# Where the last four parts of a modulation are computed: beside the chunked linear attention or beside the latent attention

## The chip, the cores and the metric

The kernel runs on one core of a Trainium2 chip. Its engines work side by side and meet through semaphores: PE (TensorE) multiplies matrices into PSUM, DVE (VectorE) and ACT (ScalarE) work element by element, POOL (GpSimd) does so too and issues some transfers, SP (SyncE) issues nearly all transfers. The metric is the time of one execution in microseconds; lower is better.

## What the kernel computes

Two transformer blocks over 512 tokens of width 1024. Only the first block matters here. Its modulation turns a vector `c` into six parts of 1024 values:

```python
sc = jax.nn.silu(c)
shift1, scale1, gate1, shift2, scale2, gate2 = jnp.split(sc @ w_mod + b_mod, 6, axis=-1)
h = modulate(rms_norm(x, norm1_g), shift1, scale1)
y, yc = token_mixer(h, hc, P, last)
x = x + gate1[:, None, :] * y
h = modulate(rms_norm(x, norm2_g), shift2, scale2)
x = x + gate2[:, None, :] * grouped_moe(h, ...)
```

`shift1` and `scale1` are needed before the token mixer, the last four parts (`gate1`, `shift2`, `scale2`, `gate2`) only after it. The token mixer has three branches: a gated linear attention, computed in chunks of 64 tokens in both directions with 4 heads; a softmax attention of 8 heads whose 512 queries see 512 + 256 keys (the latent attention); and a long convolution (hyena). A mixture of 16 experts follows, which gathers tokens into slots.

## The kernel before

The kernel is a chain of stages. Each stage is one block with an instruction list for each engine, written out by hand; every engine must have ended its list before the next stage starts. The stages that matter here, in order, with the time at which PE starts each in the profile: the first two parts of the modulation (`mod_stage`, 0), the projections of the linear attention (`gla_project_stage`, 43 us), its chunks (`gla_chunk_stage`, 165.6 us), keys, queries and values (`qk_stage`, 241.2 us), the latent attention (`latent_attention_stage`, 346.5 us) and the projections of the hyena (`hyena_project_stage`, 488.3 us).

**Weights.** `Ring` (line 49) holds four slots of 1 MB. `plan_block1` (line 3788) lists the chunks in the order of their use; SP loads chunk k once chunk k − 4 has been used. `issue_until(sp, n)` issues the list up to chunk n. A stage issues its own chunks and some of the next stage's. In the plan of before, 16 chunks named `mod2` (the last four parts of `w_mod`) stand between the query chunks and the hyena chunks.

**Split weights.** For most projections a weight chunk is split into two rounded parts: ACT copies it (`Split.high`, line 118, recorded on line 124) and POOL subtracts the copy from the chunk (`Split.low`, line 126, recorded on line 130). PE waits for the second. In `groups_stage` these are done ahead for the following group, and for the first chunks of the stage after it: `leave=1` leaves one of the two next chunks to the following stage, `leave=2` both.

**The rest of the modulation.** `LaterMods` (line 432) works in 8 groups of 512 columns. It is called with a step number a. On PE, at a mod 4 = 0 and 1, four matmuls each multiply a chunk (`mod_products`, line 316) into PSUM bank 7; at a mod 4 = 3 four small matmuls turn the row into columns (`mod_turn`, line 323). Between them ACT copies the row out of PSUM (line 463, at a mod 4 = 2); after them DVE adds the bias (line 473, at the next a mod 4 = 0). The first product of a group waits for DVE's sum of the group before (`added`), since both use the same bank. Before, this ran in the latent attention, with its steps numbered as that stage's own: one step to each of 32 blocks of 128 queries.

**The chunk stage.** First, for four pairs of direction and heads, PE multiplies chunk states (lines 263 and 1242) and DVE carries the state from chunk to chunk (lines 1316, 1321, 1326). Then come 16 heads, that is 4 token tiles by 4 heads. For head a PE computes scores (`scores(a)`, line 1255); DVE masks them (line 1333); PE computes outputs (`outputs(a)`, lines 1268 and 1274); ACT squares them (line 1299); DVE takes mean and reciprocal (lines 1342 and 1345); ACT takes the root (line 1302); DVE scales by it (line 1348) and multiplies by the gate (line 1352). `scores` runs one head ahead of `outputs`; `outputs(a)` waits until head a − 2 is done. At the end PE transposes all heads (line 1290) and ACT copies the result (line 1305). Beside this, SP wrote zeros into `h_slots`, the slots of the experts (16 transfers of 512 KB), from a region that DVE had cleared (line 1311).

**The latent attention.** For block a PE computes scores (line 1393), DVE takes the maximum (line 1442) and the bias (line 1448), ACT the exponential (line 1421), DVE normalises block a − 1 (line 1455), PE transposes block a − 2 (line 1403), DVE copies the transposes out (line 1463), and after each fourth block PE multiplies by the values (line 263) and ACT copies (line 1430).

Of the kernel before, what the change touches and what calls it, by code (L numbers as in the profile page):

```python
# [14 lines left out]
D = 1024  # L15
# [7 lines left out]
RING = 4  # L23
# [15 lines left out]
C_KV, C_GK, C_GV, C_GA = 0, 512, 768, 1280  # L39
# [547 lines left out]
def qk_stage(K):  # L587
# [2 lines left out]
    r, T = K.ring, K.T  # L590
    split = K.split1
    (raw_done, sq_done, ss_done, mean_done, rec_done, rstd_done, gained, swap_done, t1_done, t2_done, added, out_done,
     v_done, v_copied, ctx_done, zero_done, select_done, rows_done, cols_done, scale_rec) = K.signals(20)
    sq, t, t1, t2, rec = K.at(100, 2, S), K.at(104, 3, S), K.at(110, 2, S), K.at(114, 2, S), K.at(118, 2, S)
    cos, sin, swap = K.at(124, S), K.at(126, S), K.at(128, P)
    rows, select, q_rec = K.at(129, S)[0:8], K.at(131, 16), K.at(131.25, 8 * ST)
# [19 lines left out]
    with K.nc.Block() as block:  # L616
# [12 lines left out]
        @block.sync  # L629
        def _(sp):  # L630
            K.start(sp)
            r.issue_until(sp, n0 + 6 + RING)

        @block.tensor
        def _(pe):
# [155 lines left out]
        @block.vector  # L791
        def _(dve):
            def invert(j):
                ntok = items[j][0]
                m = rec[:, j % 2, 0:ntok]
                dve.wait_ge(ss_done, j + 1)
                if j >= 2:
                    dve.wait_ge(out_done, j - 1)
                dve.tensor_scalar(m, K.ps[:, 4, 0:ntok], 1.0 / P, EPS, ALU.mult, ALU.add).then_inc(mean_done, 1)
                dve.wait_ge(mean_done, j + 1)  # L800
                dve.reciprocal(m, m).then_inc(rec_done, 1)

            def context_norm(j):
                ntok, gain, _, dest = items[j]
                dve.wait_ge(rstd_done, j + 1)
                dve.scalar_tensor_tensor(dest, K.ps[:, j % 4, 0:ntok], K.vec(gain), rec[:, j % 2, 0:ntok],
                                         ALU.mult, ALU.mult).then_inc(ctx_done, 1)

            def rotate(j):
                dest, q = items[j][3], rope_no[j]  # L810
                a, b = t1[:, q % 2, :], t2[:, q % 2, :]
                dve.wait_ge(gained, q + 1)
                dve.wait_ge(K.loaded, K.loads(3))
                dve.tensor_tensor(a, t[:, q % 3, :], cos, ALU.mult).then_inc(t1_done, 1)
                dve.wait_ge(swap_done, q + 1)
                dve.tensor_tensor(b, K.ps[:, 5, :], sin, ALU.mult).then_inc(t2_done, 1)
                dve.wait_ge(t1_done, q + 1)
                dve.wait_ge(t2_done, q + 1)
                if j < NK:
                    dve.tensor_tensor(a, a, b, ALU.add).then_inc(added, 1)  # L820
                    dve.wait_ge(added, q + 1)
                    dve.wait_ge(rstd_done, j + 1)
                    dve.tensor_tensor(dest, a, rec[:, j % 2, :], ALU.mult).then_inc(out_done, 1)
                else:
                    dve.tensor_tensor(dest, a, b, ALU.add).then_inc(out_done, 1)

            invert(0)
            invert(1)
            rotate(0)
            rotate(1)  # L830
            for j in (2, 3):
                invert(j)
                context_norm(j)
            for j in range(NK, NI):
                rotate(j)
            dve.wait_ge(cols_done, 1)
            dve.tensor_scalar(q_rec.rearrange("p (h i) -> p i h", i=ST),
                              K.ps[:, 7, 0:8 * ST].rearrange("p (i h) -> p i h", h=8), 1.0 / P, EPS, ALU.mult, ALU.add)\
                .then_inc(scale_rec, 1)
            dve.wait_ge(scale_rec, 1)  # L840
            dve.reciprocal(q_rec, q_rec).then_inc(scale_rec, 1)
            dve.wait_ge(scale_rec, 2)
            dve.wait_ge(ctx_done, 2)
            dve.wait_ge(out_done, rope_no[NI])
# [170 lines left out]
def gla_project_stage(K):  # L1015

    r = K.ring
    n = r.first("ga")
    groups = [{"n": n, "items": [channel_group_item(K, 0, "act", K.ga[0:32, 0:S], 32)],
               "raw": [context_channels(K, n, 0, 32, "dve", K.ga[0:32, S:S + NCTX])]}]  # L1020
    n += 2
    groups.append({"n": n, "items": [channel_group_item(K, t * P, "act", K.gk[:, t, 0:S]) for t in range(2)],
                   "raw": [context_channels(K, n, t * P, P, "dve", K.gk[:, t, S:S + NCTX]) for t in range(2)]})
    n += 2
    groups.append({"n": n, "items": [channel_group_item(K, t * P, "act", K.gq[:, t, :], scale=0.125) for t in range(2)]})
    n += 2
    groups.append({"n": n, "items": [token_group_item(K, part_of_tokens(t), 0, 512, "act", K.gv[:, t, :])
                                     for t in range(ST)],
                   "raw": [context_tokens(K, n, t, "dve", K.gv[:, ST + t, :]) for t in range(CT)]})
    n += 2  # L1030
    groups.append({"n": n, "items": [token_group_item(K, part_of_tokens(t), 0, 512, "act", K.og[:, t, :], func=ACT.Silu)
                                     for t in range(ST)]})

    def norms(signals):
        x = NormApply(K, signals[0:3], K.xT, (K.h_hi, K.h_lo), lambda t: K.gain1[:, t:t + 1], lambda t: mod_col(K, 0, t),
                      K.rstd_x, K.at(72, KD, S))
        c = NormApply(K, signals[3:6], K.hcT, K.hcT, lambda t: K.gain1c[:, t:t + 1], lambda t: mod_col(K, 0, t, 1),
                      K.rstd_c)
        return (x, c), (r.first("ga"), r.first("ga") + 1)

    groups_stage(K, K.split1, groups, n + 2, (0, 1, 2, 7), beside=gla_decay_work, norms=norms, leave=1)

def gla_decay_work(K, signals, emptied):
# [147 lines left out]
def gla_chunk_stage(K):  # L1192

    T = K.T
    (cs_done, st_done, att_done, masked, o_done, sq_done, mean_done, rec_done, rstd_done, y_done, turned,
     copied, init_done, zeroed, cleared) = K.signals(15)
    NC = S // 64
    nothing = K.at(10, D)
    masks = K.at(0, 2, P)
    gain = K.at(1, P)  # L1200
    att = K.at(2, 2, 2, P)
# [4 lines left out]
    with K.nc.Block() as block:  # L1206
        @block.gpsimd
        def _(pool):
            pool.dma_start(masks, T["k_causal"].rearrange("d s q -> s d q")).then_inc(K.loaded, 16)
            pool.dma_start(gain, T["gla_norm_g"].broadcast_to([P, P])).then_inc(K.loaded, 16)  # L1210
            K.split1.low(K, pool, K.ring.first("kv") + 1)

        @block.sync
        def _(sp):
            K.start(sp)
            sp.wait_ge(zeroed, 1)
            for e in range(NEXP):
                sp.dma_start(K.h_slots[1 + e * SLOTS:1 + (e + 1) * SLOTS, :], nothing).then_inc(cleared, 16)
            for rows in (K.h_slots, K.y_slots):
                sp.dma_start(rows[0:1, :], nothing[0:1, :]).then_inc(cleared, 16)  # L1220
            sp.wait_ge(cleared, 16 * (NEXP + 2))

        def order(d, c):

# [3 lines left out]
        def _(pe):  # L1228
# [49 lines left out]
            for a in range(17):  # L1278
                if a < 16:
                    scores(a)  # L1280
                if a >= 1:
                    outputs(a - 1)

# [9 lines left out]

        @block.scalar
        def _(act):
            K.split1.high(K, act, K.ring.first("kv") + 1)
            for a in range(16):
                act.wait_ge(o_done, a + 1)
                act.activation(ysq[:, a % 2, :], K.ps[:, 2 + a % 2, 0:P], ACT.Square, accum_out=stats[:, 0, a:a + 1])\
                    .then_inc(sq_done, 1)  # L1300
                act.wait_ge(rec_done, a + 1)
                act.activation(stats[:, 2, a:a + 1], stats[:, 1, a:a + 1], ACT.Sqrt).then_inc(rstd_done, 1)
# [5 lines left out]

        @block.vector
        def _(dve):  # L1310
            dve.memset(nothing, 0.0).then_inc(zeroed, 1)
            for u in range(4):
                d = u // 2
                b = 3 * (u % 2)
# [21 lines left out]
            mask(0)  # L1336
            for a in range(16):
                t, h = a // 4, a % 4
                if a + 1 < 16:
                    mask(a + 1)  # L1340
                dve.wait_ge(sq_done, a + 1)
# [124 lines left out]
def latent_attention_stage(K):  # L1466

    def scores(h, i):
# [2 lines left out]

    attention_stage(K, 8, S + NCTX, scores, lambda h, j: K.v[:, j, (h // 4) * P:(h // 4 + 1) * P],
                    lambda h: K.yattT[:, h, :], None, 100, scales=K.at(Q_SCALE_AT, 8 * ST),
                    beside=lambda signals: LaterMods(K, signals, 134), issue=K.ring.first("mod2") + 16,
                    split=K.split1, first=(K.ring.first("hy"), K.ring.first("hy") + 1))

# [2310 lines left out]
def plan_block1(K):  # L3788
# [8 lines left out]
    r.add_matrix("gq", w, C_GQ, C_GQ + 256)  # L3797
    r.add_matrix("gv", w, C_GV, C_GV + 512)
    r.add_matrix("og", w, C_OG, C_OG + 512)
    r.add_matrix("kv", w, C_KV, C_KV + 512)  # L3800
    r.add_matrix("q", w, C_Q, C_Q + 1024)
    for g in range(4, 12):
        for h in range(2):
            r.add("mod2", wm[h][:, :, g * HALF:(g + 1) * HALF])
    r.add_matrix("hy", w, C_HY, C_HY + 1536)
    K.split1.add(r.first("ga"), 10)
    K.split1.add(r.first("kv"), 6)
# [132 lines left out]
```

## Time and profile before

| | |
|---|---|
| median of 3 runs | 2396.5 us (2395.36 to 2403.04) |
| the profiled execution | 2399.45 us, span 2397.6 us |
| PE busy | 2178.0 us, 91% |
| weight loads of PE (PEld) | 1633.3 us, 68% |
| DVE busy | 1128.6 us, 47% |
| ACT busy | 870.5 us, 36% |
| POOL busy | 537.4 us, 22% |
| moved | 299.68 MB, mean 125 GB/s |

### The profile page before, as it was taken

What the parts mean: (1) busy time and instruction counts of PE and PEld (TensorE: products, weight loads), DVE (VectorE), ACT (ScalarE), POOL (GpSimd) and SP (SyncE); (2) the same over time, 40 slices, a digit from 0 to 9 for tenths busy, and PEclk for the clock granted to TensorE, in tenths of its full rate; (3) what the DMA queues carried; (4) which work ended last, traced back from release to release, by engine and by line L of the source; (5) the groups of instructions that cost most, each with busy time, mean ns of one, the idle gap of its engine ahead of it and who ended that gap; (6) DMA issues with size and microseconds to landing.
All of it is one profiled execution on the core that took longest, in us unless ns stands there. A gap on an engine that the chain in (4) does not pass through costs nothing. (4 is left out here: it accounts for less than half of the span.)

```text
span 2397.6 us, 23687 instructions
## 1 busy us (share of the span) xinstructions
PE 2178.0 (91%) x9454; PEld 1633.3 (68%) x9454; DVE 1128.6 (47%) x1471; ACT 870.5 (36%) x1123; POOL 537.4 (22%) x165
## 2 busy tenths in 40 slices
PE   6999999999879999859999969899699988999997
PEld 3767855574348887748777747687378876887885
DVE  3453356734662234278888556405622245223223
ACT  4532223333113223247777536515332232211221
POOL 1320210130004444010000003430044442443440
PEclk9995999999989999879999989999799999999999
DMA  6241224321014232259999932221022233222210
GB/s 233 88 151 63 81 71 141 106 92 44 0 36 132 79 97 100 67 216 356 385 385 389 329 120 88 92 88 45 0 80 88 88 106 105 90 104 87 87 53 35
DMA packets 174846, 299.68 MB, mean 125 GB/s; under 512 B 8943, under 2 KB 66490, under 8 KB 174744
## 3 DMA queue, kind: packets, MB, share of 16 engines
q1 hardware_dynamic: 169400, 279.93, 33.6%
q0 software_dynamic: 3040, 9.93, 1.2%
q10 hardware_dynamic: 2304, 8.39, 0.9%
q8 instruction: 72, 1.18, 0.2%
q14 instruction: 30, 0.25, 0.0%
HBM read 275.10 MB, written 23.13 MB: 124 GB/s over the span
## 5 line engine op out<-in xcount | busy, mean ns | idle before, releaser
L130 POOL TENSOR_TENSOR region<-weights,region 128x2048 fp32r<-128x2048 f32 (+2 forms) x94 | 366.5, 3901 | 1057.9 <-ACT region L124 769.6
L240 PE MATMUL ps<-region 128*128 128x512 f32 (+1 forms) x1336 | 535.0, 400 | 41.7 <-DVE region L2228 11.8
L243 PE MATMUL ps<-region 128*128 128x512 f32 (+1 forms) x1336 | 520.4, 389 | 0.0
L244 PE MATMUL ps<-region 128*128 128x512 f32 (+1 forms) x1336 | 519.9, 389 | 0.0
L240 PEld LDWEIGHTS ps<-region 128*128 128x128 f32 x1336 | 259.2, 194 | 108.2 <-issue 22.3
L243 PEld LDWEIGHTS ps<-region 128*128 128x128 f32 x1336 | 259.4, 194 | 54.6 <-issue 6.5
L244 PEld LDWEIGHTS ps<-region 128*128 128x128 f32 x1336 | 258.9, 194 | 50.8
L124 ACT ACTIVATE region<-weights 128x2048 fp32r<-128x2048 f32 (+2 forms) x98 | 158.5, 1621 | 295.9 <-PE ps L244 245.0
L2716 DVE TENSOR_TENSOR region<-weights,region 128x2048 fp32r<-128x2048 f32 x96 | 218.7, 2290 | 52.5 <-ACT region L2639 52.4
L2639 ACT ACTIVATE region<-weights 128x2048 fp32r<-128x2048 f32 x96 | 183.8, 1918 | 69.5 <-DMA weights<-moe_w_up 29.8
L281 PE MATMUL ps<-region 128*128 128x512 f32 x480 | 192.0, 400 | 6.7 <-DVE region L3583 4.1
L3424 POOL TENSOR_TENSOR region<-weights,region 128x2048 fp32r<-128x2048 f32 x30 | 143.0, 4780 | 226.1 <-ACT region L3536 178.3
L283 PE MATMUL ps<-region 128*128 128x512 f32 x480 | 187.1, 390 | 0.0
L282 PE MATMUL ps<-region 128*128 128x512 f32 x480 | 186.8, 389 | 0.0
L2555 PE MATMUL ps<-region 128*128 128x512 f32 x384 | 154.9, 403 | 10.7 <-issue 8.7
L2246 DVE TENSOR_TENSOR region<-ps,region 128x512 f32<-128x512 f32 x48 | 33.1, 690 | 259.6 <-PE ps L244 259.6
L2556 PE MATMUL ps<-region 128*128 128x512 f32 x384 | 152.0, 396 | 0.0
L2557 PE MATMUL ps<-region 128*128 128x512 f32 x384 | 151.7, 395 | 0.0
L281 PEld LDWEIGHTS ps<-region 128*128 128x128 f32 x480 | 90.2, 188 | 29.9 <-DVE region L3587 6.0
L3591 DVE TENSOR_TENSOR region<-ps,region 128x512 f32<-128x512 f32 x64 | 44.3, 692 | 128.7 <-PE ps L283 128.7
L3536 ACT ACTIVATE region<-weights 128x2048 fp32r<-128x2048 f32 x32 | 60.3, 1911 | 122.1 <-PE ps L3512 118.2
L283 PEld LDWEIGHTS ps<-region 128*128 128x128 f32 x480 | 90.1, 188 | 19.1
(396 smaller groups left out, 2810.4 us busy)
## 6 DMA issues: line engine op xcount, KB each, us to landing
weights<-w_in SPq DMA_DIRECT2D x54, 1024.0 KB, 5.1
weights<-moe_w_gate SPq DMA_DIRECT2D x32, 1024.0 KB, 7.7
weights<-moe_w_up SPq DMA_DIRECT2D x32, 1024.0 KB, 8.7
weights<-moe_w_down SPq DMA_DIRECT2D x32, 1024.0 KB, 7.6
weights<-w_mod SPq DMA_DIRECT2D x24, 1024.0 KB, 5.1
weights<-w_mlp_in SPq DMA_DIRECT2D x16, 1024.0 KB, 5.2
weights<-w_mlp_out SPq DMA_DIRECT2D x16, 1024.0 KB, 5.0
h_slots<-region SPq DMA_DIRECT2D x16, 512.0 KB
```

Of the source, the lines that this page charges most:

```text
L124: act.activation(flat(self.part(K, n, 0)), flat(r.view(n)), ACT.Copy).then_inc(self.hi_done, 1)
L130: eng.tensor_tensor(flat(self.part(K, n, 1)), flat(self.ring.view(n)), flat(self.part(K, n, 0)).bitcast(F32), ALU.subtract).then_inc(self. ...
L240: ins = pe.matmul(out, l_hi, r_hi, start=(start and k == 0), stop=False)
L243: pe.matmul(out, l_hi, r_lo, start=False, stop=False)
L244: ins = pe.matmul(out, l_lo, r_hi, start=False, stop=(stop and k == kt - 1))
L281: pe.matmul(out, w_hi, x_hi, start=(n == 0), stop=False)
L282: pe.matmul(out, w_hi, x_lo, start=False, stop=False)
L283: last = pe.matmul(out, w_lo, x_hi, start=False, stop=(n == len(triples) - 1))
L2555: pe.matmul(K.ps[:, bank, :], x_hi[:, x, :], w_hi[:, k, :], start=(start and k == 0), stop=False)
L2556: pe.matmul(K.ps[:, bank, :], x_hi[:, x, :], w_lo[:, k, :], start=False, stop=False)
L2639: act.activation(flat(part(c, 0)), r.slots[n % RING][:, :], ACT.Copy).then_inc(hi_done, 1)
L2716: dve.tensor_tensor(flat(part(c, 1)), r.slots[n % RING][:, :], flat(part(c, 0)).bitcast(F32), ALU.subtract).then_inc(r.used, 1)
```

## The change

Four edits belong together. The 16 `mod2` chunks move in the plan, from behind the query chunks to ahead of the key and value chunks (`kv`). `LaterMods` is called in the 16 heads of the chunk stage, two of its steps to a head, and no longer in the latent attention. The zeroing of the slots moves from the chunk stage to the stage of keys and queries. Both key and value chunks are now rounded in the chunk stage (`leave=2`), ACT's part at heads 13 and 15, where before one was rounded at the end of the projections and one at the start of the chunk stage.

```diff
@@ qk_stage @@
+    nothing = K.at(10, D)
...
             K.start(sp)
+            sp.wait_ge(zeroed, 1)
+            for e in range(NEXP):
+                sp.dma_start(K.h_slots[1 + e * SLOTS:1 + (e + 1) * SLOTS, :], nothing).then_inc(cleared, 16)
+            for rows in (K.h_slots, K.y_slots):
+                sp.dma_start(rows[0:1, :], nothing[0:1, :]).then_inc(cleared, 16)
             r.issue_until(sp, n0 + 6 + RING)
+            sp.wait_ge(cleared, 16 * (NEXP + 2))
...
+            dve.memset(nothing, 0.0).then_inc(zeroed, 1)
             invert(0)
@@ gla_project_stage @@
-    groups_stage(K, K.split1, groups, n + 2, (0, 1, 2, 7), beside=gla_decay_work, norms=norms, leave=1)
+    groups_stage(K, K.split1, groups, n + 2, (0, 1, 2, 7), beside=gla_decay_work, norms=norms, leave=2)
@@ gla_chunk_stage @@
-    nothing = K.at(10, D)
+    mods = LaterMods(K, mod_signals, 10)
+    kv = K.ring.first("kv")
...
-            K.split1.low(K, pool, K.ring.first("kv") + 1)
+            for h in range(2):
+                K.split1.low(K, pool, kv + h)
...
             K.start(sp)
-            sp.wait_ge(zeroed, 1)
-            for e in range(NEXP):
-                sp.dma_start(K.h_slots[1 + e * SLOTS:1 + (e + 1) * SLOTS, :], nothing).then_inc(cleared, 16)
-            for rows in (K.h_slots, K.y_slots):
-                sp.dma_start(rows[0:1, :], nothing[0:1, :]).then_inc(cleared, 16)
-            sp.wait_ge(cleared, 16 * (NEXP + 2))
+            K.ring.issue_until(sp, kv + RING)
...
                 if a < 16:
                     scores(a)
+                    mods.pe(pe, 2 * a)
+                    mods.pe(pe, 2 * a + 1)
                 if a >= 1:
                     outputs(a - 1)
...
-            K.split1.high(K, act, K.ring.first("kv") + 1)
             for a in range(16):
+                mods.act(act, 2 * a + 2)
+                if a in (13, 15):
+                    K.split1.high(K, act, kv + (a - 13) // 2)
                 act.wait_ge(o_done, a + 1)
...
-            dve.memset(nothing, 0.0).then_inc(zeroed, 1)
...
                 t, h = a // 4, a % 4
+                if a % 2:
+                    mods.dve(dve, 2 * a + 2)
                 if a + 1 < 16:
                     mask(a + 1)
@@ latent_attention_stage @@
-                    beside=lambda signals: LaterMods(K, signals, 134), issue=K.ring.first("mod2") + 16,
+                    issue=K.ring.first("hy"),
@@ plan_block1 @@
-    r.add_matrix("kv", w, C_KV, C_KV + 512)
-    r.add_matrix("q", w, C_Q, C_Q + 1024)
     for g in range(4, 12):
         for h in range(2):
             r.add("mod2", wm[h][:, :, g * HALF:(g + 1) * HALF])
+    r.add_matrix("kv", w, C_KV, C_KV + 512)
+    r.add_matrix("q", w, C_Q, C_Q + 1024)
     r.add_matrix("hy", w, C_HY, C_HY + 1536)
```

## Rows read from the trace of the kernel before

**Rows 1.** Busy time by stretch; the last figures are granted clock, DMA share, GB/s.

```profile
183.40:241.20 57.80, 56.17 (x272) 43.04 (x272) 20.80 (x80) 12.80 (x53) 0.00 (x0) 0.50 0.10 40
346.50:487.90 141.40, 134.91 (x608) 71.52 (x608) 91.15 (x169) 48.12 (x83) 9.03 (x2) 0.96 0.36 119
```

**Rows 2.** Timeline of PE in the chunk stage: start us, us, engine, line.

```profile
183.40 1.08 PE L1255 MATMUL ps<-region 64*128 64x128 f32 x8 [3.27 <-DVE region L1326]
...
190.59 1.22 PE L1255 MATMUL ps<-region 64*128 64x128 f32 x4
191.74 1.22 PE L1268 MATMUL ps<-region 128*128 128x128 f32 x4
...
193.94 1.22 PE L1255 MATMUL ps<-region 64*128 64x128 f32 x4
...
236.30 3.83 PE L1290 MATMUL ps<-ident,region 128*128 128x128 f32 x16
241.24 0.76 PE L240 MATMUL ps<-region 128*128 128x512 f32 x1 [1.10 <-PEq L1206]
```

**Rows 3.** Timeline of ACT and DVE after the third head's output.

```profile
190.71 0.28 ACT L1299 ACTIVATE region<-ps 128x128 f32<-128x128 f32 x1 [1.46 <-PE ps L1274]
...
191.50 0.20 ACT L1302 ACTIVATE region<-region 128x1 f32<-128x1 f32 x1 [0.42 <-DVE region L1345]
...
192.12 0.29 DVE L1352 TENSOR_TENSOR region<-region 128x128 f32<-128x128 f32 x1
```

**Rows 4.** Timeline of PE over one attention head.

```profile
405.15 1.45 PE L1393 MATMUL ps<-region 128*128 128x512 f32 x4
406.44 0.95 PE L323 MATMUL ps<-both,region 128*128 128x2 f32 x8
407.25 0.85 PE L1403 MATMUL ps<-ident,region 128*128 128x128 f32 x6
...
409.61 1.06 PE L316 MATMUL ps<-weights,silu_c 128*32 128x512 f32 x8 [0.21 <-DVE mods L473]
410.60 0.87 PE L1403 MATMUL ps<-ident,region 128*128 128x128 f32 x6
...
421.55 1.02 PE L1393 MATMUL ps<-region 128*128 128x512 f32 x2
```

**Rows 5.** Timeline of DVE over the same head.

```profile
406.64 0.96 DVE L1442 TENSOR_REDUCE region<-ps 128x1 f32<-128x768 f32 x1 [4.39 <-PE ps L1393]
...
409.30 0.15 DVE L473 TENSOR_TENSOR mods<-ps,vec_cols 128x4 f32<-128x4 f32 x1
...
412.81 0.96 DVE L1442 TENSOR_REDUCE region<-ps 128x1 f32<-128x768 f32 x1 [0.34 <-PE ps L1393]
...
414.61 0.96 DVE L1463 COPY region<-ps 128x768 f32<-128x768 f32 x1
```

**Rows 6.** Timeline of PE at the attention's start.

```profile
348.40 1.94 PE L316 MATMUL ps<-weights,silu_c 128*32 128x512 f32 x8
```

**Rows 7.** Busy time in three stretches, with the granted clock.

```profile
343.90:347.30 3.40, 0.98 (x5) 0.58 (x5) 1.74 (x4) 1.06 (x2) 0.00 (x0) 1.00 0.00 0
347.50:350.70 3.20, 3.20 (x12) 0.88 (x11) 1.12 (x2) 1.25 (x3) 0.00 (x0) 0.50 0.01 3
350.90:353.90 3.00, 3.00 (x14) 1.02 (x13) 1.69 (x4) 0.57 (x1) 0.00 (x0) 1.00 0.79 246
```

**Rows 8.** Timeline of POOL and DVE late in the attention.

```profile
466.13 4.52 POOL L130 TENSOR_TENSOR region<-weights,region 128x2048 fp32r<-128x2048 f32 x1 [148.43 <-ACT region L124]
...
466.34 4.73 DVE L1455 TENSOR_SCALAR region<-region 128x768 f32<-128x768 f32 x1
```

**Rows 9.** Timeline of SP's queue.

```profile
166.76 17.88 SPq L1218 DMA_DIRECT2D h_slots<-region  x16
...
283.84 0.96 SPq L87 DMA_DIRECT2D weights<-w_in  x2
```

**Rows 10.** Timeline of DVE in the stage of keys and queries.

```profile
263.02 0.63 DVE L814 TENSOR_TENSOR region<-region 128x512 f32<-128x512 f32 x1
```

More of the change, by code:

```diff
@@ L592, in qk_stage @@
     (raw_done, sq_done, ss_done, mean_done, rec_done, rstd_done, gained, swap_done, t1_done, t2_done, added, out_done,
-     v_done, v_copied, ctx_done, zero_done, select_done, rows_done, cols_done, scale_rec) = K.signals(20)
+     v_done, v_copied, ctx_done, zero_done, select_done, rows_done, cols_done, scale_rec, zeroed, cleared) = K.signals(22)
+    nothing = K.at(10, D)
     sq, t, t1, t2, rec = K.at(100, 2, S), K.at(104, 3, S), K.at(110, 2, S), K.at(114, 2, S), K.at(118, 2, S)
@@ L1195, in gla_chunk_stage @@
     (cs_done, st_done, att_done, masked, o_done, sq_done, mean_done, rec_done, rstd_done, y_done, turned,
-     copied, init_done, zeroed, cleared) = K.signals(15)
+     copied, init_done, *mod_signals) = K.signals(16)
     NC = S // 64
-    nothing = K.at(10, D)
+    mods = LaterMods(K, mod_signals, 10)
+    kv = K.ring.first("kv")
     masks = K.at(0, 2, P)
```

## Prediction

> **What bounds it now.** I first read the busy time by stretch. In the chunk stage's second part (183.4 to 241.2 us) PE is busy 56.17 of 57.80 us, but at a granted clock of 0.50, the lower level, 1.2 GHz; the latent attention has 0.96 and DVE 91.15 us of 141.40 [rows 1]. The two stages between which the modulation moves are thus bound differently. Then the timelines. In the chunk stage one head's scores S (L1255) take 1.15 us (190.59 to 191.74) and its outputs O (L1268, L1274) 2.20 us (191.74 to 193.94), with no gap: PE sets the pace, 3.35 us a head, 6.7 us a pair of heads [rows 2]. Behind each O runs a chain that PE does not feel today: with O issued by 190.59, ACT's square starts at 190.71, its root at 191.50, DVE's last product ends at 192.41 [rows 3]. So root done is O + 1.1, head done O + 1.8. In the attention PE's work of the modulation, two products P (L316, 1.0 us each, 409.61 to 410.60) and one turn T (L323, 0.81 us, 406.44 to 407.25), stands in each head of 16.40 us (405.15 to 421.55) [rows 4], while DVE goes from one step to the next in 2.66 us (406.64 to 409.30) and idles little between [rows 5].
>
> The sum is made against the profiled execution: 2399.45 us, its span 2397.6 and 1.85 around it. The median of the runs is 2396.5, 3 us less; the final number goes by that.
>
> **Taken out of the attention.** Per head PE sheds 2 × 1.0 + 0.81 + the 0.21 stall = 3.0 us. DVE keeps most of it. Today the copy that lets the next transposes go starts at 414.61. Without the modulation, DVE's steps begin at 406.64, 409.30 and 411.96, and the copy 1.80 us into the last (414.61 − 412.81), at 413.76: 0.85 us a head is won [rows 5]. PE's own work then fits between the steps. The first head wins more, since its first P (1.94 us) runs at the low clock ahead of the second scores [rows 6]: about 1.5 us. With seven heads at 0.85 and some 0.4 at the end this gives −8 us. Bounds: −6, and −24 if PE alone set the pace (8 × 3.0), which [rows 5] speak against.
>
> **Put into the chunk stage.** A group of the modulation goes with each pair of heads, e even and o = e + 1. PE's order becomes: S(e), P, P, O(e−1), S(o), T, O(e), then S(e+2), P, P. Two waits are new.
>
> T waits for ACT's copy of the rows. That copy stands behind the root of head e−1, which follows O(e−1), which PE issues after the products. Root done at O + 1.1, copy 0.6 us: T starts at O + 1.8. Behind T in PE's queue stands O(e), for which the whole chain of head e waits.
>
> The next pair's first P waits for `added`, DVE's sum of the columns, which stands behind the last product of head e: O(e) + 1.8, then 0.15 for the sum [rows 5] and 0.1 to PE, say O(e) + 2.05. S(e+2) covers part of it. Queued behind P is O(o).
>
> One pair from O(e−1) to O(o): 1.8 until T, T, O(e), 2.05, two P, O(o).
> - At the low clock: 1.8 + 1.6 + 2.2 + 2.05 + 2 × 1.9 + 2.2 = 13.65 us. P is 1.94 busy there [rows 6]. A T at the low clock is in no row; between 0.81 and twice that I take twice, as P doubled.
> - At the high clock: S is 0.54 (eight instructions, two S, in 1.08) [rows 2], O half of 2.20: 1.8 + 0.8 + 1.1 + 2.05 + 2.0 + 1.1 = 8.85 us.
>
> Even the better price exceeds today's 6.7, since 3.85 us of it are waits.
>
> **Which clock.** It stood at 0.50 through all of these 57.8 us of S and O, busy as PE was [rows 1]. It rose in the attention after 3.2 us of scores and P without a gap at 0.50 (347.5 to 350.7), so the products count as work. It had fallen at the end of a stretch with 0.98 us of matmuls in 3.40 [rows 7]. Two P make 3.8 us without a gap, so I expect rises in about two pairs of three. Between O(e−1) and the next P, at the high clock, PE does S 0.54, idles 1.2, does T (two columns each), O 1.1, S 0.54 and idles 1.5: about as thin as what stood ahead of that fall. So I expect it to fall again in every pair, and P to run low. A rise at the end of P then buys one O (1.1) and perhaps one T (0.8), in two of three pairs: 13.65 − 0.65 × 1.8 = 12.5 us a pair. This is the choice on which the number hangs.
>
> The Trainium skill (TensorE: Matmul & The Clock Gate, Part 1) says that throttled is the default and "activity releases the throttle". By that alone the products would free the loop for good, 8.85 us a pair; rows 7 show the fall that it leaves out here. It is the second rival below.
>
> **The sum of the stage.** S(0) starts at 183.40 as before; it waits for DVE's states, which lose only a memset and a POOL subtraction beside them. First pair: S to 184.5, P to 188.3, T from 189.4 (copy) to 191.0, O(0) to 193.2. Its head is done 2.7 later, the first root loading a table (about 0.9 more than later ones), `added` 0.3 after, P until 200.0, O(1) at 202. Six pairs to O(13): 75, at 277.
>
> The tail has both roundings of the key and value matrix. ACT's second one (1.9 us) follows root(14), then POOL subtracts 4.5 us. From O(13): T at 1.8 to 3.4, O(14) 5.6, O(15) 7.8, root(14) 6.7, rounding to 8.6, POOL 8.7 to 13.3. POOL's subtraction holds DVE: at 466.13 it took 4.52 us, and a DVE instruction of the kind that takes 0.6 us, begun at 466.34, took 4.73 [rows 8]. Head 15's chain starts at 9.1, within it, so it ends at 13.3 + 1.3 = 14.6. Four transposes (0.24 each, 3.83 for 16 [rows 2]), ACT's copy 0.6 and 0.5 to the next stage: 16.7. Keys start at 294, not at 241.24 [rows 2]: +53 us. If DVE's one-column instructions pass and only the product with two SBUF inputs is held, it is 1 us less. The Trainium skill (GPSIMD Engine Reference, 1. Specifications) names exactly these as contending: two-port modes or two SBUF inputs. By it alone the sum is the same, since head 15 has such a product.
>
> **Costs nothing.** The 16 loads of 1 MB: at the 246 GB/s of [rows 7] two take 8.5 us, under any pair above, and four slots run ahead; without that cover each group would wait up to 8.5 us. The key and value chunks take the slots that the seventh group's products free, 6 us or more ahead of ACT's first rounding. Zeroing: SP issues 16 writes in 17.88 us and two more in 1.5; in the stage of keys SP next has to load 42.6 us after the start (283.84 − 241.24) [rows 2, 9]. The tables by POOL's queue now travel beside the writes; DVE first needs them at 263.02, 21.8 us in [rows 10]; if they come behind all writes it is 1 to 2 us. The memset (under 1 us) lies ahead of DVE's first work. The hyena chunks arrive during keys and queries, earlier than needed.
>
> Total: +53 − 8 = +45: 2444.5 by this execution, 2441 against the median.
>
> **Rivals.**
> 1. The clock never rises: 202 + 6 × 13.65 + 17 = 301, +60 − 8 = +52, 2448. For it: 57.8 us at 0.50. Against: [rows 7].
> 2. The clock rises with the first products and stays: O(1) at 196.5, six pairs 53, tail 17: 266.5, +25.5 − 8 = +17.5, 2414. For it: products are dense. Against: thin work between them. A clock held over half the pairs gives about 2428.
> 3. Faster: the clock rises and the copy and sum are never last. A pair then costs 2 × (0.54 + 1.1) + 2.0 + 0.8 = 6.1, under 6.7; keys start at 234 to 241, and with −8 the time is about 2385. It decides once rows copied come ahead of S(o)'s end and `added` ahead of S(e+2)'s. Against it stands the written order: each copy is behind the root of a head whose O follows the products.
> 4. All hidden, no change: chunk stage +8 only, i.e. a pair of 7.2; needs the same.
>
> **Chances.** Forecast (clock up and down) 0.6; never up 0.17; mostly up, or half the pairs, 0.18; faster 0.03; no change 0.02. Range 2414 to 2452: the upper end has T and P at full low-clock cost plus 4 us for loads or tables, the lower the held clock; about one in ten is left out. The likeliest case's own range is 2432 to 2447. Over 0.3% (7 us) is what a measurement of this kernel tells from no change: slower 0.95, same 0.02, faster 0.03.
>
> **What will show it.** T (L323) with an idle of about 0.6 us (low clock) to 1.2 us (high) released by ACT's copy, and the first P of a group with 0.9 to 1.5 us released by DVE's sum, seven times; pairs of 12 to 13.6 us; a granted clock of 0.5 to 0.7 in the loop; one DVE instruction near the stage's end stretched to over 4 us beside POOL; the attention about 8 us shorter; keys and queries the same length. Wrong if the loop's clock is near 1.0, if products wait for loads, or if the attention's heads fall by more than 1 us each.

## The result and the profile after

| | before | after |
|---|---|---|
| median | 2399.77 us (2395.36 to 2408.09, 4 runs) | 2444.72 us (2440.78 to 2451.34, 4 runs) |
| the profiled execution | 2399.45 us, span 2397.6 | 2440.78 us, span 2439.0 |

After takes 1.018 of the time of before, 95% interval 1.0153 to 1.0207: 1.8% slower. The forecast was 2441, in a range of 2414 to 2452. All ratios of this document leave out an execution that took over 1.5% longer than the fastest of its kernel, which are one of e4 (2406.45 us) and one of e5 (8694.91 us).

The timeline of PE gives the start of each stage. Nearly all of the 41.4 us between the two spans is in the chunk stage:

| from, to | before | after | difference | forecast |
|---|---|---|---|---|
| start to the first scores S(0) | 183.40 | 187.44 | +4.0 | 0 |
| S(0) to keys and queries | 57.84 | 102.36 | +44.5 | +53 |
| keys and queries | 105.26 | 105.12 | −0.1 | 0 |
| latent attention | 141.79 | 134.64 | −7.15 | −8 |
| rest | | | +0.1 | 0 |

The busy time by stretch in the kernel after, to be read beside [rows 1] (the last three figures are the granted clock, the DMA share and GB/s): the loop with its tail, then four stretches inside it, then the attention.

```profile
187.40:289.80 102.40, 85.59 (x465) 52.25 (x465) 24.68 (x89) 20.07 (x63) 9.02 (x2) 0.63 0.48 165
204.80:225.20 20.40, 18.34 (x89) 10.71 (x88) 4.02 (x17) 2.20 (x10) 0.00 (x0) 0.50 0.38 130
225.30:228.40 3.10, 2.17 (x20) 1.45 (x16) 0.79 (x4) 1.06 (x4) 0.00 (x0) 1.00 0.92 303
228.60:238.70 10.10, 9.28 (x44) 5.54 (x44) 1.67 (x7) 0.57 (x3) 0.00 (x0) 0.50 0.43 137
238.80:242.20 3.40, 2.46 (x23) 2.00 (x22) 1.30 (x5) 1.06 (x4) 0.00 (x0) 0.99 1.03 395
394.90:529.50 134.60, 114.39 (x416) 62.78 (x416) 83.67 (x160) 44.15 (x75) 9.28 (x2) 0.95 0.00 1
```

PE idles 16.8 of 102.4 us there, against 1.6 of 57.8 before, and its clock alternates: in most pairs it goes up near the end of a group's products and is down again some 3 us later. The chain of waits says for whom it idles (engine, line and what it waited for: us in total, times, longest). L316 is a product, L323 the turn, L463 ACT's copy of the rows, L473 DVE's sum, L1297 the transposes at the end.

```profile
PE ps L316 <- DVE mods L473: 7.1, 7, 2.2
PE ps L323 <- ACT region L463: 6.0, 7, 0.9
PE ps L1260 <- DVE region L1334: 3.3, 1, 3.3
PE ps L1297 <- DVE region L1362: 2.1, 1, 2.1
```

The first two rows are the two waits that the change adds, seven times each. The third was there before (3.27 us ahead of S(0), [rows 2]). One pair of heads on PE's timeline (start, duration), where [rows 2] had S and O (here L1260 and L1273, L1279) without a gap:

```profile
226.76 0.71 PE L1260 MATMUL ps<-region 64*128 64x128 f32 x4
228.40 1.79 PE L323 MATMUL ps<-both,region 128*128 128x2 f32 x8 [0.94 <-ACT region L463]
230.05 1.20 PE L1273 MATMUL ps<-region 128*128 128x128 f32 x4
231.18 1.12 PE L1279 MATMUL ps<-region 64*64 64x128 f32 x8
232.23 1.22 PE L1260 MATMUL ps<-region 64*128 64x128 f32 x4
234.27 3.64 PE L316 MATMUL ps<-weights,silu_c 128*32 128x512 f32 x16 [0.82 <-DVE mods L473]
237.84 1.14 PE L1273 MATMUL ps<-region 128*128 128x128 f32 x4
238.90 0.65 PE L1279 MATMUL ps<-region 64*64 64x128 f32 x8
```

Read it with the clock: the scores of 226.76 and O before them are at the high level (0.71 for four instructions), PE idles 0.94, the clock falls at about 228.5, and T, O, S and both products run at the low one (1.79, 1.20, 1.12, 1.22, 3.64). The products bring it up again, just as they end: the next O's second half takes 0.65. In the pair from 202.12 they did not: the second row of the busy times, which starts behind that pair's turn, is a stretch of 20.4 us at 0.50. From O(1) at 202.12 to O(13) at 274.48 six pairs take 72.36 us, 12.06 each.

The tail, DVE's timeline while POOL subtracts (its subtraction ran from 282.89 for 4.51 us):

```profile
283.17 0.15 DVE L1352 TENSOR_SCALAR region<-region 128x1 f32<-128x1 f32 x1 [1.18 <-ACT region L1308]
283.36 0.16 DVE L1355 RECIPROCAL region<-region 128x1 f32<-128x1 f32 x1
283.79 0.35 DVE L1358 SCALAR_TENSOR_TENSOR region<-ps,region 128x128 f32<-128x128 f32 x1 [0.27 <-ACT region L1311]
284.18 3.37 DVE L1362 TENSOR_TENSOR region<-region 128x128 f32<-128x128 f32 x1
```

Three instructions pass POOL undisturbed; the product with both inputs in SBUF, 0.29 us elsewhere [rows 3], takes 3.37. The last transposes wait 2.12 us for it.

### The profile page after: what moved, and what is told of

It reads as the page before. It is cut to its first block and busy times, and to the rows that moved or that the text cites. A ratio compares the mean times of both kernels' runs of the same rounds, so it can differ in the third digit from the quotient of the medians.

```text
span 2439.0 us, 23687 instructions
## 1 busy us (share of the span) xinstructions
PE 2195.9 (90%) x9454; PEld 1636.6 (67%) x9454; DVE 1124.6 (46%) x1471; ACT 869.9 (36%) x1123; POOL 537.1 (22%) x165
```

## The experiments

My theory: the cost is the two waits, by their own length and by letting the clock fall in every pair. The main rival: it is PE's added work itself, and would be there without a wait. Both get a part: e2 and e9 bear on the first, e7 beside e10 on the second. Further runs ask after the small parts, and how the loop of before came to run at the low clock.

All numbers below "S(0) to keys" are from one profiled run of each kernel, and the medians of before differ by a few us between chips, so each kernel has its ratio to before on the same chip.

| kernel | median, us | ratio to before, 95% interval | S(0) to keys, us | clock there |
|---|---|---|---|---|
| before | | | 57.84 | 0.50 |
| after | 2444.72 | 1.018 (1.0153 to 1.0207) | 102.36 | 0.63 |
| e1: after, own bank | 2428.11 | 1.0107 (1.0061 to 1.0153) | 90.94 | 0.67 |
| e9: after, late turn | 2407.85 | 1.0028 (1.0015 to 1.0041) | 68.87 | 0.90 |
| e2: after, both | 2406.57 | 1.0028 (1.0007 to 1.0048) | 66.62 | 0.83 |
| e7: after, both, spread, products ahead | 2398.46 | 0.9984 (0.9966 to 1.0002) | 62.18 | 0.94 |
| e3: after, waits filled | 2422.95 | 1.0104 (1.0075 to 1.0133) | 80.67 | 0.95 |
| e5: before, zeroing moved | 2400.63 | 0.9991 (0.9973 to 1.001) | 57.38 | 0.52 |
| e6: before, roundings moved | 2404.70 | 1.0014 (0.9999 to 1.0029) | 61.38 | 0.50 |
| e4: before, products ahead | 2378.20 | 0.9913 (0.988 to 0.9945) | 54.01 | 0.56 |
| e11: the same again | 2387.65 | 0.9955 (0.9923 to 0.9987) | 34.74 | 1.00 |
| e8: before, ahead and 256 wide in each head | 2385.67 | 0.9936 (0.9919 to 0.9954) | 40.89 | 1.00 |
| e10: the same, 64 wide | 2382.11 | 0.9913 (0.9898 to 0.9929) | 37.76 | 1.00 |

**e1, a bank of its own for the turn.** The first product no longer has to wait for DVE's sum.

```diff
-                pe.wait_ge(self.added, g)
+                pe.wait_ge(self.rows_copied, g)
...
-            mod_turn(K, pe, self.rows, self.BANK, 0).then_inc(self.turned, 1)
+            if g >= 1:
+                pe.wait_ge(self.added, g)
+            mod_turn(K, pe, self.rows, 6, 0).then_inc(self.turned, 1)
...
-            pv = K.ps[:, self.BANK, 0:8].rearrange("p (j b) -> p j b", b=2)
+            pv = K.ps[:, 6, 0:8].rearrange("p (j b) -> p j b", b=2)
```

> The changed kernel, but the turn writes PSUM bank 6, so the first product of a group waits for ACT's copy of the row and no longer for DVE's sum. Theory (two waits behind the head chain, and a clock that falls in them): the first wait, before the turn, stays (0.4 us at the low clock, 0.94 at the high); the second, 0.82 us before each of six groups and 2.2 before the second, is gone: the loop gets 6 to 9 us shorter, 2436 to 2439 where the changed kernel has 2444.7, unless the clock's falls shift by one stretch. Rival (the wait is only the visible end of a chain that would hold the outputs anyway): the idle time moves behind the products and the time stays within 3 us of the changed kernel.

2428.11 us. The wait for the sum is gone from the loop, the one for the copy is as it was. The two largest rows of PE's waits, from the first scores on (the others are in the tail, 3.5 us together):

```profile
PE ps L323 <- ACT region L465: 6.6, 7, 0.9
PE ps L1262 <- DVE region L1336: 3.3, 1, 3.3
```

It won 16.6 us by the medians, where I expected 6 to 9, and 11.4 in the profiled stage, where the wait itself had been 7.1. That a wait costs more than its length fits this, but is not well shown by it: the four runs of e1 lie 19 us apart. The removal alone did not keep the clock up. It still fell in each pair but the first, with the turn's wait as it was.

**e2, own bank and the turn behind the outputs of the even head.** As e1, and:

```diff
-                    mods.pe(pe, 2 * a)
-                    mods.pe(pe, 2 * a + 1)
+                    if a % 2 == 0:
+                        mods.pe(pe, 2 * a)
+                        mods.pe(pe, 2 * a + 1)
                 if a >= 1:
                     outputs(a - 1)
+                if a < 16 and a % 2:
+                    mods.pe(pe, 2 * a + 1)
```

> As before, and the turn is issued behind the outputs of the even head, when ACT's copy is long done. Theory: both waits are gone; seven more pairs lose 0.4 to 0.94 us, 3 to 6 us less than with the bank alone, 2431 to 2435. Rival 1 (the price is the work at the low clock, not the waits): within 3 us of the version with the bank alone. Rival 2 (without idle time the clock holds at the high level): pairs near 7 us in place of 12, and 2405 to 2412.

2406.57 us, where my theory had 2431 to 2435: rival 2 came. PE has no wait in the loop; at the high clock a pair with the same work takes 6.56 us (from the scores of 213.07 to those of 219.63). So most of what after loses is the order: with the same added work the stage is 8.8 us longer than before, not 44.5. That the work costs nothing is not shown by this, for in e2 it also raises the clock at which scores and outputs run (e7 compares at one clock). The clock fell all the same, at about 201.5, 235.5 and, at the last outputs, 245.9, each time right behind a turn and with no gap ahead of it; behind the other turns it did not.

```profile
213.07 0.71 PE L1262 MATMUL ps<-region 64*128 64x128 f32 x4
213.71 0.71 PE L1275 MATMUL ps<-region 128*128 128x128 f32 x4
214.35 0.65 PE L1281 MATMUL ps<-region 64*64 64x128 f32 x8
214.93 1.05 PE L323 MATMUL ps<-both,region 128*128 128x2 f32 x8
215.92 0.71 PE L1262 MATMUL ps<-region 64*128 64x128 f32 x4
216.56 1.93 PE L316 MATMUL ps<-weights,silu_c 128*32 128x512 f32 x16
218.41 0.71 PE L1275 MATMUL ps<-region 128*128 128x128 f32 x4
219.05 0.65 PE L1281 MATMUL ps<-region 64*64 64x128 f32 x8
219.63 0.71 PE L1262 MATMUL ps<-region 64*128 64x128 f32 x4
```

**e9, the late turn alone,** the second diff without the first, so the bank is shared.

> The changed kernel, with the turn of a part issued behind the outputs of the even head in place of ahead of them, and nothing else: the bank is still shared, so the next part's first product still waits for DVE's sum. It completes the square with the version with its own bank (2428.1) and the one with both (2406.6). Theory (each wait lets the clock fall, so one wait that is left still costs most of the second gain): the turn's seven waits of 0.9 us go (6.6 us), while the first products' waits stay or grow, the clock still falls in most pairs, 2430 to 2440. Rival (the waits are additive and the turn's place is worth what it was with a bank of its own, 21.5 us): 2420 to 2426. Second rival (DVE's sum comes as much later as the turn does, and the first product waits longer by the same): 2441 to 2446.

2407.85 us: 36.9 us from the place of one instruction group, where I expected 5 to 15, and nothing left for the bank to win. All three expectations missed. PE's waits in its loop and tail:

```profile
PE ps L1260 <- DVE region L1337: 3.3, 1, 3.3
PE ps L316 <- DVE mods L473: 2.9, 6, 1.2
PE ps L1300 <- DVE region L1365: 2.6, 1, 2.6
PE ps L1300 <- ACT region L1317: 1.5, 1, 1.5
```

The turn's waits are gone, as expected, but the products' waits fell too, from 7.1 to 2.9 us (0.34 each once the loop runs):

```profile
200.78 0.65 PE L1279 MATMUL ps<-region 64*64 64x128 f32 x8
201.36 1.05 PE L323 MATMUL ps<-both,region 128*128 128x2 f32 x8
202.35 0.71 PE L1260 MATMUL ps<-region 64*128 64x128 f32 x4
203.40 1.92 PE L316 MATMUL ps<-weights,silu_c 128*32 128x512 f32 x16 [0.34 <-DVE mods L473]
```

From where PE is through with O(e) to the product it is 2.04 us, here (201.36 to 203.40) as in after (232.23 to 234.27): that is the chain of head e with DVE's sum behind it. In after only the scores lie in this time; in e9 T does too, and fills what was idle. With 0.34 us of idle in a pair of 6.98 us (from a T at 201.36 to the next at 208.34) the clock stayed up for most of the loop, 0.90 over it; it fell once within the products (at 225.2) and once behind a turn (at 232.0). The two gains do not add: 16.6 for the bank, 36.9 for the turn, 38.2 for both.

**e3, unused products in the waits.** After, with an unused 128x512 product behind the scores of heads 1 to 15 (`filler` multiplies into a bank that nobody reads).

```diff
                     scores(a)
+                    if a >= 1:
+                        filler(K, pe, 512)
```

> The changed kernel with one more matmul of 128x128 by 128x512 (result unused, PSUM bank 6) behind the scores of each of heads 1 to 15, so that PE has work where it waited. It adds 15 matmuls, 0.85 us each at the high clock and 1.7 at the low. Theory (the clock falls because PE's work between the products is thin): the clock holds at the high level after the first products, pairs go from 12.06 to about 8.9 us plus 0.85 or less for what doesn't fit the waits: 9 to 9.8 us, the loop 14 to 20 us shorter, 2425 to 2431. Rival (the clock does not follow such work, or falls for another reason): the clock still falls in every pair, each matmul costs up to 1.7 us less the wait it fills, and the time is 2450 to 2460.

2422.95 us, 2 us below what I expected: with fifteen more products it is 22 us faster than after. This separates the clock from the waits: the chain from copy to T and from sum to product is as before, but the clock stays up from 191.75 to 263.25, and a pair takes 8.88 us (216.42 to 225.30), against a forecast of 8.85 for a pair at the high clock. It shows what the clock costs; that the idle time is what lets it fall is argued, since the unused products are also more work.

```profile
216.42 1.92 PE L316 MATMUL ps<-weights,silu_c 128*32 128x512 f32 x16 [0.27 <-DVE mods L479]
...
225.30 1.92 PE L316 MATMUL ps<-weights,silu_c 128*32 128x512 f32 x16 [0.27 <-DVE mods L479]
```

**e5, the zeroing alone,** in the kernel before: the 18 transfers and the memset in the keys' stage, with the lines of the change.

> The kernel before, with one part of the change alone: the zeroing of the slots and its memset move from the chunk stage to the keys-and-queries stage. The prediction's step costs this at nothing: the 18 transfers are issued on SP's queue while nothing on it is due, and the memset is one short DVE instruction. Theory: within 2 us of the kernel before (ratio 0.999 to 1.001). Rival: the transfers delay the loads behind them on the queue or the keys' first DVE work, and the keys' stage (105.4 us from 241.24 to 346.50 before) grows by 3 us or more; then some of the 44.5 us found in the chunk stage's window would not be the modulation's.

2400.63 against 2401.89, ratio 0.9991: the zeroing costs nothing measurable. The keys' stage took 103.45 us (241.41 to 344.86), no longer than before. The rival is out.

**e6, both roundings in the chunk stage alone,** in the kernel before: `leave=2`, `high` at heads 13 and 15, `low` twice.

> The kernel before, with the other small part alone: both halves of the keys' and values' weights are rounded inside the chunk stage, on ScalarE at heads 13 and 15 and on POOL, in place of one half there and one in the stage before. Theory: the heads' chain DVE to ACT to DVE is touched in two heads, by one ScalarE rounding and POOL's subtraction each; POOL's 4.5 us subtraction held one DVE instruction 3.37 us in the changed kernel, so 2 to 7 us more (ratio 1.001 to 1.003), all between the last heads and the keys. Rival: it is hidden, since TensorE alone bounds the heads here (56.17 of 57.80 us busy), within 1.5 us of before.

2404.70 against 2401.89, +2.8 us, the interval just reaching no change (ratio 1.0014, 0.9999 to 1.0029). In the profile S(0) to keys is 3.5 us longer, and DVE's timeline shows where. Both of POOL's subtractions (232.54 and 239.89, 4.5 us each) stretch the product with two SBUF inputs, and no other DVE instruction:

```profile
233.40 0.15 DVE L1344 TENSOR_SCALAR region<-region 128x1 f32<-128x1 f32 x1 [1.71 <-ACT region L1301]
...
234.41 2.77 DVE L1354 TENSOR_TENSOR region<-region 128x128 f32<-128x128 f32 x1
...
241.30 3.25 DVE L1354 TENSOR_TENSOR region<-region 128x128 f32<-128x128 f32 x1
```

**e4 and e11, the clock of the loop before.** Before, PE idles 3.27 us ahead of S(0) and the clock falls at 183.75, as the first scores start. Four unused products fill that gap:

```diff
+            filler(K, pe, 512, 512, 512, 256)
+
             def scores(a):
```

> The kernel before, with four unused matmuls (128x512 three times, 128x256 once, 3.0 us together at the high clock) in the 3.27 us in which PE waits for DVE ahead of the first scores. Theory (scores and outputs ran at 1.2 GHz for 57 us only because the clock fell in that wait, and their own work is enough to hold it but not to raise it): the granted clock of the loop is near 1.0, a head costs 1.8 to 2.2 us in place of 3.35, then bound by DVE's and ACT's chain, and the stage loses 18 to 24 us: 2376 to 2382 where before has 2399.8. Rival (this work is too thin to hold the clock as well): it falls within some 10 us, and the time is 2395 to 2400.

> The kernel before with the four unused products ahead of the first scores alone, a second time: its times spread from 2368.3 to 2406.5 and its one profile fell in a run at 2406.45, where the clock fell at 190.75. Theory (scores and outputs alone neither raise the clock nor hold it reliably): spread of over 20 us again, and the profile shows high clock for a part of the loop that fits its time, 28 us for the whole loop at most. Rival (the low run was an outlier): all runs within 8 us at 2368 to 2380.

Medians 2378.20 and 2387.65 us. The profiled run of e4 was its slowest (2406.45 us, 27 us over the next): there the clock fell at 190.75, within the scores and outputs, and stayed down to the end of the loop. That of e11 (2380.84 us) had it up throughout. The ratio of e11 (0.9955), in which three executions of over 2406 us stand, is the fairer one for this kernel. Busy time by stretch, two of e4 and one of e11:

```profile
183.70:190.60 6.90, 5.77 (x53) 4.39 (x53) 3.01 (x12) 2.40 (x7) 0.00 (x0) 1.00 0.83 340
190.80:237.70 46.90, 45.84 (x220) 35.10 (x219) 17.48 (x69) 10.27 (x46) 0.00 (x0) 0.50 0.00 1
```
```profile
185.50:220.20 34.70, 31.62 (x272) 24.40 (x272) 20.69 (x80) 12.45 (x53) 0.00 (x0) 1.00 0.18 71
```

The same 272 matmuls take 57.8 us [rows 1] or 34.7 us. At the low clock they don't raise it, though PE is 97% busy; at the high one they can hold it, though PE is only 91% busy, but not in each execution: the 12 runs of e11 lie from 2373.94 to 2407.65 us. Their mean clock over the whole execution is 0.952 to 0.959 in the six below 2383 us and 0.940 to 0.941 in the three above 2406.

**e8 and e10, an unused product in each head as well,** 256 and 64 columns wide.

```diff
                     scores(a)
+                    filler(K, pe, 256)
```

> The kernel before, with four unused products ahead of the first scores and one unused 128x256 product behind the scores of each head. Theory (the chunk loop before runs at the low clock for its whole length, though TensorE is busy 56.17 of 57.80 us, and it stays high once it is high and kept so): clock high in the whole loop, heads about 1.9 to 2.1 us, the loop 30 to 34 us in place of 57.8, 2368 to 2376 in every run. Rival (S and O alone decide, the one extra product is too little): falls to low within the loop in some runs, as the version without the extra product did in its profiled one (190.75), median 2376 to 2406 with wide spread.

> The kernel before, with four unused products ahead of the first scores and one unused 128x64 product behind the scores of each head, a quarter of the width of the version at 2385.7 us, whose heads took 2.29 us of which the unused product was 0.60. Theory (any product in every head keeps the clock high; its width only costs): heads of 1.85 to 2.0 us, the loop from first scores to the keys 35 to 37 us in place of 40.9, 2377 to 2382 with a spread like the wider one's (6 us). Rival (the width is what keeps it high): the clock falls within the loop in some runs, spread over 20 us as without any product in the heads.

2385.67 us (2384.55 to 2390.22) and 2382.11 us (2378.33 to 2387.91). Both have a clock of 1.00 from S(0) to the keys, and their runs stay within 6 and 10 us. I had the size wrong in e8: a head takes 2.29 us, 0.43 more than the 1.86 of e11, for PE sets the pace there too, so the loop took 40.9 us, not 30 to 34. In e10 a head takes 2.08 us and the loop 37.8, just above what I gave it.

```profile
200.58 0.71 PE L1263 MATMUL ps<-region 64*128 64x128 f32 x4
201.22 0.43 PE L435 MATMUL ps<-region,ones 128*128 128x64 f32 x2
201.49 0.66 PE L1276 MATMUL ps<-region 128*128 128x128 f32 x4
202.08 0.65 PE L1282 MATMUL ps<-region 64*64 64x128 f32 x8
202.66 0.71 PE L1263 MATMUL ps<-region 64*128 64x128 f32 x4
```

e10 beats both kernels: 0.9913 of before (0.9898 to 0.9929). Against e11, without a product in the heads, it is the spread that is clearly smaller (9.6 us for 33.7); the intervals of the two ratios overlap.

**e7, the best that I could make of the change.** Own bank, products ahead of the first scores, one product to a head in place of two to each second head, and the turn two heads later (DVE's sum moves with it):

```diff
                     scores(a)
-                    mods.pe(pe, 2 * a)
-                    mods.pe(pe, 2 * a + 1)
+                if a >= 2 and a % 2 == 0:
+                    mods.pe(pe, 2 * a - 1)
+                if a < 16:
+                    mods.pe(pe, 4 * (a // 2) + a % 2)
```

> The changed kernel, with the turn in a bank of its own, the first product of a part waiting only for ScalarE's copy of the rows, the products spread one part per two heads with the turn behind the scores of the next head but one, and four unused products ahead of the first scores. Theory (the two waits and the clock that they let fall are the cost): no wait of TensorE inside the loop, clock high from the first scores on, pairs of heads 6.1 to 6.6 us, the loop 52 us, 2390 to 2402. Rival (the products themselves cost more than the waits): no better than the version with a late turn and a bank of its own, 2404 to 2410.

2398.46 us, in the range, but the loop took 62.2 us, not 52: I had left out the tail (8 us from the last outputs) and put a pair at 6.1 to 6.6, it takes 6.70. The clock was up from S(0) to 243.25. It is 0.9984 of before, no measurable difference, and it answers the main rival. With the clock up in nearly all of both loops, S(0) to keys takes 37.8 us without the modulation (e10) and 62.2 with it (e7), 24.4 more. These 24.4 hold the two roundings (3.5 us in e6's profile) and a low clock in e7's last 7 us, and leave out e10's sixteen unused products. The pairs alone say nearly the same: 6.70 us against two heads of 1.86 in e11, 3.0 a pair, 24 in eight. So the products and turns do cost about 24 us of PE's time at the high clock, for 7 that the attention gives back. Beside a loop that the clock favours the move loses too.

## Why the prediction was right

**Attention, −8.** Measured −7.15. A head went from 16.40 us [rows 4] to 15.52 (PE's scores at 417.94 and 433.46), 0.88 less where 0.85 was forecast from DVE's steps; PE now waits for DVE's copy of the transposes (L1473) 24 times, 17.6 us in all. PE shed 20.5 us of busy time there (134.91 to 114.39) and the stage 7: it had been DVE's pace, as [rows 5] had it, that set the time.

**Pair of heads, 12.5.** Measured 12.06, over six pairs 72.4 for 75. Both waits came where they were placed, seven times: T for ACT's copy 0.94 us where the scores ahead of it ran at the high clock (forecast 1.2) and 0.43 in the one pair where they ran at the low (forecast 0.6), the first product for DVE's sum 0.82 (forecast 0.9 at the low clock), 2.22 in the first of the seven. The two prices that no row had were near: T 1.79 us at the low clock (forecast 1.6), two products 3.64 (forecast 3.8). The prices at the high clock were read too low: one S takes 0.64 us in e2, not 0.54, one O 1.22, not 1.1. The 1.08 us of [rows 2] are eight instructions issued in one go while the clock was falling (183.75), and no price for one S.

**The clock, up and down.** Right, with one size off: of the six pairs from O(1) to O(13) it rose in five, where two of three was forecast, and each time it fell again in the next pair, in its turn or right behind it. The one pair without a rise, from 202.12, started high and fell at about 204.8. The reason given for the fall, that PE's work is thin between the outputs and the next product, has e3 and e9 behind it: fill the waits, or take the turn's away, and the clock stays up for most of the loop. In e1, with one wait of 0.94 us per pair, it fell in seven of eight pairs; in e9, with one of 0.34, in two. What decides the single fall stays open, for e2 has falls without any wait.

**First pair, 18.6.** Measured 14.68 (S(0) at 187.44, O(1) at 202.12). The clock rose within the first two products (3.12 us, not 3.8) and held until 197.75; the step had all of the pair at the low level.

**Tail, 16.7.** Measured 15.3. The case named last in that step came: the one-column instructions pass POOL, the product with two SBUF inputs is held, 1 us less. The Trainium skill (GPSIMD Engine Reference, 1. Specifications) has DVE instructions with two SBUF inputs contend with GpSimd; the traces of after and of e6 agree, with 3.37, 2.77 and 3.25 us for 0.29.

**What was priced at nothing.** The loads: no product waits for one. The zeroing: e5. The roundings were in the tail's price; alone they cost 2.8 us in e6.

**What the sum left out.** S(0) comes 4.0 us later, most of it from earlier stages: the chunk stage starts at 168.9, not 165.6. Whether this is the change's is open. The clock is low in stretches of those stages that differ from run to run, and kernels that are alike up to that point show the same spread: the chunk stage started at 165.5 in e8 and at 170.3 in e10. But in all six profiles of kernels with the change it started at 168.9 to 169.4, and in six of the seven without it at 165.5 to 167.7. No run here separates the two.

By terms: 44.5 for 53, −7.15 for −8, +4.0 for 0, 41.4 in all for 45. Two errors of 8 and 4 us partly cancel, and the second was no part of the sum: without it the profiled difference would be 37.4 (worked out, not measured). The stage is 8 us shorter than forecast, as each of its parts was put too high: the first pair by 3.9, the six pairs by 2.6, the tail by 1.4. The medians differ by 45.0 us, just the forecast; that is partly luck.

**The rivals.** "The clock never rises" (2448) is out by the profile. "The clock rises and stays" (2414) is not what after did, but it is e3, whose pair of 8.88 us is the 8.85 of that rival. "Faster" (2385) named the right condition, copy and sum never last, and e2 meets it: its pair took 6.56 us where 6.1 was forecast, by the low prices of S and O. It still came out at 2406.6. The pair of before (6.7) was hardly longer than 6.56, and with its two falls of the clock the six pairs of e2 took 44.2 us (198.31 to 242.48), against 40.2 before (190.59 to 230.75); the first pair took 3.5 us more than before, the tail 1.3.

## What to carry to other kernels

Before work is moved beside a loop, find what holds that loop up: here it was PE at half its clock, where each moved microsecond counts nearly double (a turn 1.79 us for 1.05), while in the attention DVE set the pace and PE had room. Then look at where each wait falls in the instruction order: one turn placed ahead of the outputs instead of behind them made 37 of the 45 us, by its wait and by the clock that fell with it. And look at the granted clock ahead of a long dense loop; the gap of 3.3 us before this one cost 13 us by the medians of e11 and 23 by its profile, and unused products, four in the gap and a small one per head (e10), won 18.8 us with nothing else changed.

## What the runs showed of the hardware

- The same loop of 272 small matmuls stands at either clock: 57.8 us at 0.50 with PE 97% busy, 34.7 us at 1.00 with PE 91% busy. The level at which it is entered is mostly kept; a fall inside it is seen in e4 (190.75), and a rise in e5 only at the closing transposes (about 238.7).
- The Trainium skill (TensorE: Matmul & The Clock Gate, Part 1) has it that activity releases the throttle. No such release came in 57.8 us of scores and outputs before; it came with the modulation's products, in all pairs of after but one. The same section also has a fall, after idle time, which the prediction's remark on it passed over; in after the clock fell six times behind an idle of no more than 0.94 us.
- Adding work can save time: 15 unused 128x512 products made after 21.8 us faster (e3).
- In the chunk stage POOL's subtraction of two 128x2048 tiles held only the DVE instruction with two SBUF inputs (0.29 us became 2.77 to 3.37); one-column instructions and one with an input in PSUM took their usual time. In the attention before, it held a 768-column DVE instruction with one tensor input too, for 4.73 us [rows 8].
- In e2 the clock fell three times (201.5, 235.5 and 245.9) between first scores and last outputs without idle time, each time right behind a turn, whose matmuls have two columns each. Other turns of the same loop were followed by no fall. What decides stays open.
